# Positions added first on VectorE and gate weights issued later by ScalarE, at the head of a hybrid RG-LRU / GLA / PEER step

## The chip, the cores and the metric

The kernel runs on one core of one Trainium2 chip. The metric is the device time of one execution in microseconds; the time before is the median of three runs, 2560.03 us (2547.81 to 2565.61).

## The reference

One inference step of a two-layer model over 384 tokens of width 1024: 128 prompt tokens and 256 sample tokens. Only the sample tokens get a position table added before the first layer. Layer 0 mixes tokens with a bidirectional RG-LRU, layer 1 with a gated linear attention (GLA), and each layer ends with a PEER mixer that gathers 8 x 16 rows of two tables per token. All of it is float32. What the head of the program computes:

```python
xs = x_sample + grid_pos_embed(rows, D)                 # positions, sample tokens only
mod = silu(cond) @ ada_w[l] + ada_b[l]                  # six vectors of 1024 per layer and kind of token
h = rmsnorm(x, norm1_g) * (1 + scale) + shift           # pre_mod
proj = h @ w_in                                         # RG-LRU: 1024 -> 2048
xr = centred_conv(proj[..., 1024:], conv_w, conv_b)     # four taps
r = sigmoid(block_diag(xr, wa, ba)); i = sigmoid(block_diag(xr, wi, bi))    # gate weights: 16 blocks of 64 x 64
log_a = -8 * r * softplus(-lam)                         # the decay; softplus(-lam) depends on weights alone
a = exp(log_a); b = sqrt(-expm1(2 * log_a)) * (i * xr); h = linear_scan(a, b, h0)
```

## The kernel before, in words

The activations lie feature-major in SBUF: `xT` holds 8 chunks (`C`) of 128 features by 384 tokens. Each engine runs one program written out by hand, in order, and waits on semaphores.

**Weights.** SP streams the large weights as slabs of 1 MB (`stream`, L422): `SEQ` fixes their order (eight `ada` slabs, then `rg_in` 0, four `ada` slabs, `rg_in` 1, and so on) and six slab buffers take turns, so slab k is issued when slab k - 6 has been used. `ada` slabs 0 to 5 go out at once. `ada` 6 and 7 wait for `ada` 0 and 1 to be used.

**TensorE at the head.** `ada_slabs(4)` (L853, four slabs of the modulation product side by side), then `square_sum(0, c)` for the 8 chunks (L878, the norm's sum of squares), then four more `ada` slabs, `ada_columns(0)` (L868, transposes), then `project("rg_in", n)` (L946) for n = 0 to 7 with four `ada` slabs after each second one, then the gate matmuls (L1165), which first wait for all eight loads of gate weights (`bd_in`). A float32 matmul shows as two records in the trace.

**ScalarE at the head.** It issues loads itself: `vec`, `xT`, the position table, `ident`, `iota`, `wz`, and then the gate weights (L539): 8 loads of 128 KB, each in runs of 64 numbers (256 bytes) into the block-diagonal buffer `bd`, behind a wait for that buffer's zeroing. After these come Abs and Exp of lambda (L542, L543), which release VectorE's decay chain; then `squares(0)` (L557) of each chunk of x, the square root (`deviation`, L563), the copy of the first modulation rows (`rows(0)`, L550), `modulate(0)` (L575, writes `hT`) and the copies of the projections out of PSUM into `xpad` (L776, L777).

**VectorE at the head.** First the decay chain (L1227 to L1240): 25 tiny operations on 128 x 16 for softplus(-lam), whose results `dec4` and `ndec8` are first used by ScalarE's Tanh (L796). Then the position adds (L1246, 8 of 128 x 256), each of which releases one of ScalarE's squares; then `norm(0)` (L1274 reciprocal, L1276), `modulation(0)` (L1258, L1268), the zeroing of `xpad` (L1567), and the convolutions (L1571, L1574), one chunk for each copied projection.

**The rest.** Scans, output projection, layer 0's queries, and then, from about 270 us, 768 gathers of 128 rows from each of the two PEER tables, issued by GpSimd and consumed by VectorE (dot products, L1520) and TensorE (weighted sums, L1126), with layer 1's GLA laid in between. A gather waits for indices that VectorE chose.

Of the kernel before, what the change touches and what calls it, by code (L numbers as in the profile page):

```python
# [7 lines left out]
C = D // P  # L8
# [26 lines left out]
for _n in range(TOPK * NT * PH * 2):  # L35
# [3 lines left out]
RG_C = 8.0  # L39
# [6 lines left out]
ALU = mybir.AluOpType  # L46
ACT = mybir.ActivationFunctionType
# [4 lines left out]
V_CW, V_CB, V_BA, V_BI, V_LAM, V_H0, V_BAL, V_GNG, V_FG, V_EPS, V_END = (  # L52
    144, 176, 184, 200, 216, 232, 248, 256, 264, 272, 273)
# [178 lines left out]
def build(nc, x_t, pos_t, vecs, ident_d, mask_d, iota_d, keys_t, ada_w, peer_wq, peer_u, peer_v, rg_w_in,  # L232
          rg_wa, rg_wi, rg_w_out, gla_w_in, gla_w_z, w_alpha, state_gla, gla_w_out, y_t, st_rg, st_gla):
    ctx = ExitStack()
    with ctx:
        def sb(name, shape, dt=F32):
            return ctx.enter_context(nc.sbuf_tensor(name, shape, dt))
# [3 lines left out]
        def sem(name):  # L241
            if name not in sems:
                sems[name] = ctx.enter_context(nc.semaphore(name))
            return sems[name]
# [4 lines left out]
        vec = sb("vec", [P, V_END])  # L249
# [9 lines left out]
        lamv = sb("lamv", [P, 5, 2 * C])  # L259
        dec4 = sb("dec4", [P, 2 * C])  # L260
        ndec8 = sb("ndec8", [P, 2 * C])
# [4 lines left out]
        def part(at, size):  # L266
            return big[:, at:at + size]
# [14 lines left out]
        bd = bd_flat.rearrange("p (k c m) -> p k c m", k=4, c=C)  # L282
# [240 lines left out]
        def _(act):  # L523
            link = Chain(act, sem("act_step"))
# [7 lines left out]
            act.dma_start(ident[:, :], ident_d).then_inc(const_in, 16)  # L532
            act.dma_start(iota16[:, :], iota_d).then_inc(const_in, 16)
            act.dma_start(wz[:, :, :], gla_w_z).then_inc(sem("wz_in"), 16)
            act.wait_ge(sem("bd_zero"), 1)
            for kind, w in enumerate((rg_wa, rg_wi)):
                for d in range(2):
                    for half in range(2):
                        act.dma_start(bd[64 * half:64 * half + 64, 2 * d + kind, :, 64 * half:64 * half + 64],  # L539
                                      w[0, d].rearrange("(c two) i j -> two i c j", two=2)[half]).then_inc(bd_in, 16)  # L540

            link(act.activation(lamv[:, 0, :], vec[:, V_LAM:V_LAM + 2 * C], ACT.Abs))  # L542
            act.activation(lamv[:, 1, :], lamv[:, 0, :], ACT.Exp, scale=-1.0).then_inc(sem("lam_exp"), 1)  # L543

            def rows(group):

                act.wait_ge(sem("ada_used"), 8 * (group + 1))
                if group:
                    act.wait_ge(sem("ada_cols"), group)
                act.activation(ada_rows, bank[5 + group % 3], ACT.Copy).then_inc(sem("ada_rows"), 1)  # L550
# [15 lines left out]
            def modulate(n):  # L566

                k = min(n, 1)
                act.wait_ge(sem("gs_ready"), k + 1)
                for c in range(C):  # L570
                    if c % 2 == 0:
                        act.wait_ge(sem("xn_ready"), 4 * n + c // 2 + 1)
                    for s, (a, b) in enumerate(SEG):
                        if n in (0, 2 - s):
                            act.activation((hP0 if n else hT)[:, c, a:b], xn_p[:, c, :] if n == 2 else xn[:, c, a:b],  # L575
                                           ACT.Identity, scale=gs_of[0][:, k, c, s:s + 1],
                                           bias=mods_of[0][:, 3 * k * C + c, s:s + 1]).then_inc(sem("h_ready"), 1)
# [192 lines left out]
            deviation(0)  # L770
            rows(0)
            modulate(0)
            act.wait_ge(sem("xpad_zero"), 1)
            for n in range(C):
                act.wait_ge(sem("rg_in_mm"), n + 1)
                act.activation(xpad[:, n, PAD_L:PAD_L + TP], bank[n % 4][:, 0:TP], ACT.Copy)  # L776
                act.activation(xpad[:, n, S0 + PAD_L:S0 + PAD_L + TS], bank[n % 4][:, TP:T], ACT.Copy  # L777
                               ).then_inc(sem("rg_in_ev"), 1)
            rows(1)
            for d in range(2):  # L780
                if d == 1:
                    rows(2)
                for kind, dst, col in ((0, g_a[d], V_BA), (1, g_i[d], V_BI)):
                    for c in range(C):
                        n = (2 * d + kind) * C + c
# [436 lines left out]
        def _(dve):  # L1222
            link = Chain(dve, sem("dve_step"))


            dve.wait_ge(sem("lam_exp"), 1)
            e, den, w, w2, s = (lamv[:, i, :] for i in (1, 2, 3, 4, 0))  # L1227
            link(dve.tensor_scalar(den, e, 2.0, None, ALU.add))
            link(dve.reciprocal(den, den))
            link(dve.tensor_tensor(w, e, den, ALU.mult))  # L1230
            link(dve.tensor_tensor(w2, w, w, ALU.mult))
            link(dve.tensor_scalar(s, w2, 1.0 / 17, 1.0 / 15, ALU.mult, ALU.add))
            for k in (13, 11, 9, 7, 5, 3, 1):
                link(dve.tensor_tensor(s, s, w2, ALU.mult))
                link(dve.tensor_scalar(s, s, 1.0 / k, None, ALU.add))
            link(dve.tensor_tensor(s, s, w, ALU.mult))
            link(dve.tensor_scalar(den, vec[:, V_LAM:V_LAM + 2 * C], -1.0, 0.0, ALU.mult, ALU.max))
            link(dve.scalar_tensor_tensor(s, s, 2.0, den, ALU.mult, ALU.add))
            dve.tensor_scalar(ndec8[:, :], s, -RG_C, None, ALU.mult)
            dve.tensor_scalar(dec4[:, :], s, RG_C / 2, None, ALU.mult).then_inc(sem("dec_ready"), 1)  # L1240


            dve.wait_ge(x_in, 16)
            dve.wait_ge(pos_in, 16)
            for c in range(C):
# [3 lines left out]
            def modulation(group):  # L1249

                dve.wait_ge(sem("ada_cols"), group + 1)
                layer = group // 3
                mods = mods_of[layer]
                for i in range(2):
                    m = group % 3 * 2 + i
                    b = vec[:, V_ADAB + layer * 48 + m * C:V_ADAB + layer * 48 + (m + 1) * C]
                    src = bank[4][:, i * SW:(i + 1) * SW].rearrange("p (f s x) -> p s f x", f=2, s=4)[:, :, :, 0:2]
                    ins = dve.tensor_tensor(mods[:, m * C:(m + 1) * C, :].rearrange("p (s f) x -> p s f x", f=2), src,  # L1258
                                            b.rearrange("p (s f) -> p s f", f=2).unsqueeze(3).to_broadcast([P, 4, 2, 2]),
                                            ALU.add)  # L1260
                ins.then_inc(sem("ada_mod"), 1)
                if group % 3 != 1:
                    part = group % 3 // 2
                    dve.wait_ge(sem("ada_mod"), group + 1)
                    col = (V_N1, V_N2)[part]
                    g = vec[:, col + layer * C:col + (layer + 1) * C].unsqueeze(2).to_broadcast([P, C, 2])
                    r = (1 + 3 * part) * C
                    dve.scalar_tensor_tensor(gs_of[layer][:, part, :, :], mods[:, r:r + C, :], 1.0, g, ALU.add,  # L1268
                                             ALU.mult).then_inc(sem("gs_ready"), 1)
# [295 lines left out]
            norm(0)  # L1565
            modulation(0)
            dve.memset(part(6144, C * WPAD), 0.0).then_inc(sem("xpad_zero"), 1)  # L1567
            for c in range(C):
                dve.wait_ge(sem("rg_in_ev"), c + 1)
                cw = [vec[:, V_CW + c * 4 + j:V_CW + c * 4 + j + 1] for j in range(4)]  # L1570
                link(dve.tensor_scalar(xr[:, c, :], xpad[:, c, 0:WX], cw[0], vec[:, V_CB + c:V_CB + c + 1], ALU.mult,  # L1571
                                       ALU.add))
                for j in range(1, 4):
                    ins = dve.scalar_tensor_tensor(xr[:, c, :], xpad[:, c, j:j + WX], cw[j], xr[:, c, :], ALU.mult,  # L1574
                                                   ALU.add)
                    if j < 3:
                        link(ins)
                ins.then_inc(sem("xr_ready"), 1)
# [113 lines left out]
```

## Time and profile before

| | |
|---|---|
| median of three runs | 2560.03 us |
| lowest, highest | 2547.81, 2565.61 us |
| the profiled execution's own time | 2561.2 us |
| its span, first to last instruction | 2558.8 us |
| TensorE busy | 2025.1 us (79%) |
| VectorE busy | 1655.2 us (65%) |
| GpSimd busy | 1625.5 us (64%) |
| ScalarE busy | 525.5 us (21%) |
| mean granted TensorE clock | 0.894 of full speed |

The times below are microseconds from the start of the span. PE is TensorE and PEld its weight loads, DVE is VectorE, ACT ScalarE, POOL GpSimd; a q behind a name (ACTq, SPq) is the issuing of DMAs by that engine, which is not counted as busy. [...] Queue q1 carries what SP issues, q10 what ScalarE issues.

### The profile page before, as it was taken

To read this page: it belongs to the slowest core of one execution; us is meant where nothing else is said; L and a number is where in the kernel's file an instruction comes from. 1 tells how busy PE (TensorE), PEld (TensorE's weight loads), DVE (VectorE), ACT (ScalarE), POOL (GpSimd) and SP (SyncE) were. 2 spreads that over 40 slices of the span, in tenths; PEclk is the share of its full clock that TensorE was granted. 3 is DMA by queue.
4 is the path that set the end of the run, shared out by engine and by line. 5 is a ranking of instruction groups with operands and counts; after the bars stand their busy time and mean duration, and the time that the engine had idled before them with its cause. 6 is when DMAs were issued, how large, how long until landed. Compare 5 with 4: busy or idle time off the path is not lost.

```text
span 2558.8 us, 22158 instructions
## 1 busy us (share of the span) xinstructions
PE 2025.1 (79%) x6920; PEld 1102.8 (43%) x6920; DVE 1655.2 (65%) x4012; ACT 525.5 (21%) x1334; POOL 1625.5 (64%) x1543
## 2 busy tenths in 40 slices
PE   5998897977796767986686887889687776858676
PEld 2557543433342323763464465455333332424233
DVE  2235767787778756578878746576757594665744
ACT  2261211111111112221121221222111111212011
POOL 0000577777777777677776655576777777777773
PEclk8999898988898879897898899999889888988888
DMA  8884799999999999999999989899999999999996
GB/s 293 329 317 183 298 378 407 409 383 409 407 394 406 392 396 362 394 385 335 342 391 347 411 330 397 306 381 351 397 389 410 385 375 398 390 367 386 409 384 253
DMA packets 248098, 938.63 MB, mean 367 GB/s; under 512 B 31344, under 2 KB 35824, under 8 KB 232624
## 3 DMA queue, kind: packets, MB, share of 16 engines
q0 software_dynamic: 221184, 805.40, 81.2%
q1 hardware_dynamic: 19248, 125.32, 12.6%
q10 hardware_dynamic: 7552, 6.51, 0.8%
q8 instruction: 57, 0.93, 0.1%
q14 instruction: 57, 0.47, 0.1%
HBM read 934.49 MB, written 2.63 MB: 366 GB/s over the span
## 4 chain that ended last, share of the span: by engine, by line
PE 31%; POOL 29%; DMA 16%; DVE 11%; issue 11%; ACT 1%; ACTq 1%; SPq 0%; DVEq 0%; POOLq 0%
POOL big L501 22%; PE psum L1126 17%; DMA big<-in_peer_u,idx 14%; POOL big L509 7%; PE psum L946 4%; DVE big L1520 3%; DMA big<-in_peer_v,idx 2%; PE psum L1009 1%; PE psum L968 1%; PE psum L853 1%; PE psum L1049 1%; PE psum L1165 1%; ACTq L539 1%; DVE big L1494 1%; PE psum L894 1%
## 5 line engine op out<-in xcount | busy, mean ns | idle before, releaser
L1126 PE MATMUL psum<-big,diag 128*128 128x512 f32 x2816 | 1317.8, 626 | 387.9 <-ACT diag L764 369.8
L1520 DVE SCALAR_TENSOR_TENSOR big<-big 128x1024 f32<-128x1024 f32 x768 | 932.2, 1225 | 554.3 <-DMA big<-in_peer_u,idx 536.0
L501 POOL DMA_INDIRECT big<-in_peer_u,idx x768 | 823.0, 1072 | 546.0 <-DVE flag L1346 268.2
L1126 PEld LDWEIGHTS psum<-big,diag 128*128 128x128 f32 x2816 | 559.0, 202 | 1095.2 <-issue 1039.6
L509 POOL DMA_INDIRECT big<-in_peer_v,idx x768 | 798.5, 1040 | 357.0 <-issue 191.0
L764 ACT ACTIVATE diag<-ident,wts 128x128 f32<-128x128 f32 x704 | 245.0, 394 | 460.1 <-PE psum L1126 442.5
L754 ACT ACTIVATE tanh<-inner 128x16 f32<-128x16 f32 x48 | 10.4, 216 | 852.4 <-DVE inner L1528 852.4
L968 PE MATMUL psum<-big 128*128 128x128 f32 (+2 forms) x736 | 164.9, 384 | 22.1 <-ACT big L622 13.0
L968 PEld LDWEIGHTS psum<-big 128*128 128x128 f32 x736 | 123.8, 195 | 66.7 <-issue 22.9
L946 PE MATMUL psum<-big 128*128 128x384 f32 (+2 forms) x512 | 133.7, 421 | 9.8 <-DVE big L1607 6.5
L1009 PE MATMUL psum<-big 128*128 128x256 f32 (+1 forms) x768 | 131.5, 332 | 4.0 <-DMA big<-in_gla_w_in 2.3
L1009 PEld LDWEIGHTS psum<-big 128*128 128x128 f32 x768 | 118.6, 194 | 21.3 <-issue 10.7
L946 PEld LDWEIGHTS psum<-big 128*128 128x128 f32 x512 | 89.5, 197 | 51.2 <-issue 14.3
L1494 DVE SCALAR_TENSOR_TENSOR big<-big,wts 128x1024 f32<-128x1024 f32 x63 | 80.9, 1284 | 41.3 <-DMA big<-in_peer_v,idx 37.6
L1520 DVE DVE_READ_ACCUMULATOR big<-big 128x1 f32 x768 | 63.1, 82 | 0.0
L853 PE MATMUL psum<-big,cond 128*2 128x256 f32 x768 | 51.6, 398 | 8.6 <-DMA big<-in_ada_w 8.6
L607 ACT ACTIVATE big<-psum 128x256 f32<-128x256 f32 (+2 forms) x46 | 17.1, 377 | 182.0 <-PE psum L968 182.0
L1049 PE MATMUL psum<-big 128*128 128x256 f32 x192 | 42.4, 379 | 0.0
L1363 DVE SCALAR_TENSOR_TENSOR xT<-psum,mods,xT 128x256 f32<-128x256 f32 (+1 forms) x48 | 17.0, 409 | 36.0 <-PE psum L1019 35.9
L1049 PEld LDWEIGHTS psum<-big 128*128 128x128 f32 x192 | 36.5, 190 | 7.5 <-issue 2.9
L853 PEld LDWEIGHTS psum<-big,cond 128*2 128x2 f32 x768 | 20.6, 87 | 42.2 <-DMA big<-in_ada_w 13.2
L1341 DVE TENSOR_TENSOR onehot<-onehot,i 128x512 f32<-128x512 f32 x48 | 33.3, 693 | 1.6
(192 smaller groups left out, 1308.5 us busy)
## 6 DMA issues: line engine op xcount, KB each, us to landing
big<-in_ada_w SPq DMA_DIRECT2D x48, 1024.0 KB, 8.2
big<-in_peer_wq SPq DMA_DIRECT2D x24, 1024.0 KB, 8.1
big<-in_gla_w_in SPq DMA_DIRECT2D x24, 1024.0 KB, 8.2
big<-in_peer_u,idx POOLq DMA_INDIRECT x768, 6.6
big<-in_peer_v,idx POOLq DMA_INDIRECT x768, 6.8
big<-in_rg_w_in SPq DMA_DIRECT2D x8, 1024.0 KB, 11.1
big<-in_gla_w_out SPq DMA_DIRECT2D x8, 1024.0 KB, 8.5
big<-in_rg_w_out SPq DMA_DIRECT2D x4, 1024.0 KB, 7.1
```

Of the source, the lines that this page charges most:

```text
L501: pool.indirect_dma_start(ubuf[n % US], None, u_rows, bass.IndirectOffsetOnAxis(ap=idx[kept(g)][:, j:j + 1], axis=0)).then_inc(u_in[n % US ...
L509: pool.indirect_dma_start(vbuf[n % VS], None, v_rows, bass.IndirectOffsetOnAxis(ap=idx[kept(g)][:, j:j + 1], axis=0)).then_inc(v_in[n % VS ...
L764: act.activation(diag[k % DS][:, :], ident[:, :], ACT.Copy, scale=wts[g % 3][:, j:j + 1]).then_inc(sem("diag_ready"), 1)
L853: mm = pe.matmul(out[32 * s:32 * s + 2, o:o + SW], cond[:, c, :], slab[SLOT[k]][:, c, :], start=False, stop=(c == C - 1), skip_group_check ...
L946: mm = pe.matmul(out, slab[SLOT[k]][:, c, (n % 2) * P:(n % 2 + 1) * P], rhs[:, c, :], start=(c == 0), stop=(c == C - 1))
L968: mm = pe.matmul(bank[6 + half][:, 0:width], weights[:, c, half * P:(half + 1) * P], rhs[:, c, :], start=(c == 0), stop=(c == C - 1))
L1009: mm = pe.matmul(out[:, j * n:(j + 1) * n], weights[:, c, j % 2 * P:(j % 2 + 1) * P], rhs[:, c, :], start=(c == 0), stop=(c == C - 1), ski ...
L1049: mm = pe.matmul(out[:, t * DV:(t + 1) * DV], s.hT[:, c, t * P:(t + 1) * P], weights[:, c, :], start=(c == 0), stop=(c == C - 1), skip_gro ...
L1126: mm = pe.matmul(acc[t][:, half * 512:(half + 1) * 512], diag[k % DS][:, :], vbuf[n % VS][:, half * 512:(half + 1) * 512], start=False, st ...
L1341: link(dve.tensor_tensor(oh, oh, i12[:, :, :].unsqueeze(2).to_broadcast([P, 2, TOPK, TOPK]), ALU.mult))
L1494: dve.scalar_tensor_tensor(total, vbuf[n % VS], wts[g % 3][:, j:j + 1], total, ALU.mult, ALU.add).then_inc(side_done, 1)
L1520: dve.scalar_tensor_tensor(ubuf[n % US], ubuf[n % US], 0.5, x, ALU.mult, ALU.mult, accum_out=dot[:, j:j + 1]).then_inc(u_free, 1)
```

## The change

On ScalarE, the eight loads of gate weights leave the head. They are issued in pairs behind the copies of projections 0 to 3: `gate_weights(n // 2, n % 2)`. Abs and Exp of lambda move from ahead of the squares to behind `modulate(0)`. On VectorE, the decay chain moves from the start of the program to behind the zeroing of `xpad`, ahead of the first convolution, so the position adds come first.

```diff
@@ ScalarE
-            act.wait_ge(sem("bd_zero"), 1)
-            for kind, w in enumerate((rg_wa, rg_wi)):
-                for d in range(2):
-                    for half in range(2):
-                        act.dma_start(bd[64 * half:64 * half + 64, 2 * d + kind, :, 64 * half:64 * half + 64],
-                                      w[0, d].rearrange("(c two) i j -> two i c j", two=2)[half]).then_inc(bd_in, 16)
-
-            link(act.activation(lamv[:, 0, :], vec[:, V_LAM:V_LAM + 2 * C], ACT.Abs))
-            act.activation(lamv[:, 1, :], lamv[:, 0, :], ACT.Exp, scale=-1.0).then_inc(sem("lam_exp"), 1)
+
+            def gate_weights(kind, d):
+
+                w = (rg_wa, rg_wi)[kind]
+                if (kind, d) == (0, 0):
+                    act.wait_ge(sem("bd_zero"), 1)
+                for half in range(2):
+                    act.dma_start(bd[64 * half:64 * half + 64, 2 * d + kind, :, 64 * half:64 * half + 64],
+                                  w[0, d].rearrange("(c two) i j -> two i c j", two=2)[half]).then_inc(bd_in, 16)
...
             modulate(0)
+            link(act.activation(lamv[:, 0, :], vec[:, V_LAM:V_LAM + 2 * C], ACT.Abs))
+            act.activation(lamv[:, 1, :], lamv[:, 0, :], ACT.Exp, scale=-1.0).then_inc(sem("lam_exp"), 1)
             act.wait_ge(sem("xpad_zero"), 1)
             for n in range(C):
                 act.wait_ge(sem("rg_in_mm"), n + 1)
...
                                ).then_inc(sem("rg_in_ev"), 1)
+                if n < 4:
+                    gate_weights(n // 2, n % 2)
             rows(1)
@@ VectorE
             link = Chain(dve, sem("dve_step"))
-
-
-            dve.wait_ge(sem("lam_exp"), 1)
-            e, den, w, w2, s = (lamv[:, i, :] for i in (1, 2, 3, 4, 0))
...
-            dve.tensor_scalar(ndec8[:, :], s, -RG_C, None, ALU.mult)
-            dve.tensor_scalar(dec4[:, :], s, RG_C / 2, None, ALU.mult).then_inc(sem("dec_ready"), 1)
...
             dve.memset(part(6144, C * WPAD), 0.0).then_inc(sem("xpad_zero"), 1)
+            dve.wait_ge(sem("lam_exp"), 1)
+            e, den, w, w2, s = (lamv[:, i, :] for i in (1, 2, 3, 4, 0))
...
+            dve.tensor_scalar(ndec8[:, :], s, -RG_C, None, ALU.mult)
+            dve.tensor_scalar(dec4[:, :], s, RG_C / 2, None, ALU.mult).then_inc(sem("dec_ready"), 1)
             for c in range(C):
                 dve.wait_ge(sem("rg_in_ev"), c + 1)
```

The order on ScalarE from its last small load to the square root, before: gate weights (`in_rg_wa`, `in_rg_wi`) and lambda (`lamv`) stand ahead of the squares (L557).

```order
L534 DMA wz<-in_gla_w_z 128x256
L539 DMA big<-in_rg_wa 64x8x64 x4
L539 DMA big<-in_rg_wi 64x8x64 x4
L542 ACTIVATE lamv<-vec 128x16
L543 ACT_TABLE_LOAD
L543 ACTIVATE lamv<-lamv 128x16
L557 ACTIVATE big<-xT 128x384 x8
L563 ACT_TABLE_LOAD
```

The same stretch of ScalarE in the changed kernel:

```order
L533 DMA iota<-in_iota 128x16
L534 DMA wz<-in_gla_w_z 128x256
L557 ACTIVATE big<-xT 128x384 x8
L563 ACT_TABLE_LOAD
L563 ACTIVATE sd<-psum,vec 128x384
```

The squares follow the last small load directly.

ScalarE in the changed kernel from the end of `modulate(0)` (last row of L575) to the fourth projection's copies (L778 and L779, which are L776 and L777 before):

```order
L575 ACTIVATE big<-big,mods,gs 128x256
L773 ACTIVATE lamv<-vec 128x16
L774 ACT_TABLE_LOAD
L774 ACTIVATE lamv<-lamv 128x16
L778 ACTIVATE big<-psum 128x128
L779 ACTIVATE big<-psum 128x256
L542 DMA big<-in_rg_wa 64x8x64 x2
L778 ACTIVATE big<-psum 128x128
L779 ACTIVATE big<-psum 128x256
L542 DMA big<-in_rg_wa 64x8x64 x2
L778 ACTIVATE big<-psum 128x128
L779 ACTIVATE big<-psum 128x256
```

Lambda with its table load now stands between the modulation and the first copy, and two loads stand behind each of the first copies (two more pairs, of `in_rg_wi`, follow).

VectorE's first rows before, from the decay chain's last operations (`ndec`, `dec`) to the zeroing of `xpad` (L1567) and the first convolution:

```order
L1239 TENSOR_SCALAR ndec<-lamv 128x16
L1240 TENSOR_SCALAR dec<-lamv 128x16
L1246 TENSOR_TENSOR xT<-xT,big 128x256 x8
L1274 RECIPROCAL rstd<-sd 128x384
L1276 TENSOR_TENSOR big<-xT,rstd 128x768 x4
L1258 TENSOR_TENSOR mods<-psum,vec 128x16 x2
L1268 SCALAR_TENSOR_TENSOR gs<-mods,vec 128x16
L1567 MEMSET big 128x3120
L1571 TENSOR_SCALAR big<-big,vec 128x387
```

VectorE's first rows in the changed kernel, as far as the decay chain's first operations:

```order
L1233 TENSOR_TENSOR xT<-xT,big 128x256 x8
L1261 RECIPROCAL rstd<-sd 128x384
L1263 TENSOR_TENSOR big<-xT,rstd 128x768 x4
L1245 TENSOR_TENSOR mods<-psum,vec 128x16 x2
L1255 SCALAR_TENSOR_TENSOR gs<-mods,vec 128x16
L1554 MEMSET big 128x3120
L1557 TENSOR_SCALAR lamv<-lamv 128x16
L1558 RECIPROCAL lamv<-lamv 128x16
```

The adds are VectorE's first work, and the whole chain stands between the zeroing and the first convolution. TensorE's and SP's own orders are the same in both kernels.

## Rows read from the trace of the kernel before

**Rows 1.** The page: chain that ended last, share of the span by engine

```profile
PE 31%; POOL 29%; DMA 16%; DVE 11%; issue 11%; ACT 1%; ACTq 1%; SPq 0%; DVEq 0%; POOLq 0%
```

**Rows 2.** Chain of waits, 0 to 130 us: start, length, what

```profile
10.11 12.83 ACTq L539
```

**Rows 3.** Waits, 0 to 60 us: us in total, times, longest

```profile
DVE lamv L1228 <- ACT lamv L543: 29.8, 1, 29.8
```

**Rows 4.** Timeline, 0 to 100 us: start, length, engine, line, count [idle before]

```profile
1.68 0.45 ACTq L527 DMA_DIRECT2D big<-in_pos_t  x1
...
7.97 14.97 ACTq L539 DMA_DIRECT2D big<-in_rg_wa  x4
...
20.31 6.49 PE L853 MATMUL psum<-big,cond 128*2 128x256 f32 x58 [1.70 <-DMA big<-in_ada_w]
...
28.06 0.22 ACT L542 ACTIVATE lamv<-vec 128x16 f32<-128x16 f32 x1 [21.23 <-issue]
...
34.67 2.77 DVE L1246 TENSOR_TENSOR xT<-xT,big 128x256 f32<-128x256 f32 x8
35.12 3.41 ACT L557 ACTIVATE big<-xT 128x384 f32<-128x384 f32 x8 [5.32 <-DVE xT L1246]
...
35.70 7.45 PE L878 MATMUL psum<-big,ones 128*128 128x384 f32 x16 [8.90 <-ACT big L557]
...
43.08 3.64 PE L853 MATMUL psum<-big,cond 128*2 128x256 f32 x64
...
47.51 0.65 PE L868 MATMUL psum<-ident,small 128*128 128x128 f32 x4 [0.80 <-ACT small L550]
...
49.87 0.24 DVE L1258 TENSOR_TENSOR mods<-psum,vec 128x16 f32<-128x16 f32 x2
...
51.49 13.23 PE L946 MATMUL psum<-big 128*128 128x384 f32 x32 [3.32 <-ACT big L575]
...
59.65 0.28 ACT L776 ACTIVATE big<-psum 128x128 f32<-128x128 f32 x1 [2.17 <-PE psum L946]
...
69.26 10.59 PE L946 MATMUL psum<-big 128*128 128x384 f32 x32
```

**Rows 5.** DMA issues, 0 to 120 us: KB, median us to landing

```profile
xT<-in_x_t ACTq DMA_DIRECT2D x1, 1536.0 KB, 11.6
big<-in_pos_t ACTq DMA_DIRECT2D x1, 1024.0 KB, 16.1
```

**Rows 6.** Windows: length, busy of PE, PEld, DVE, ACT, POOL, granted clock, DMA share, GB/s

```profile
26.80:29.70 2.90, 0.00 (x1) 0.00 (x0) 0.00 (x0) 1.61 (x3) 0.00 (x0) 0.98 1.24 225
...
35.70:39.90 4.20, 4.20 (x7) 2.38 (x8) 1.74 (x6) 4.12 (x8) 0.00 (x0) 0.51 1.04 395
...
64.70:114.00 49.30, 49.22 (x357) 25.64 (x356) 16.45 (x28) 5.64 (x16) 0.00 (x0) 1.00 0.89 337
```

**Rows 7.** Line 853, 20.3 to 26.8 us: ns min/median/max, first and last start

```profile
L853 PE MATMUL psum<-big,cond x58: 379/631/631, 20.3 to 26.4; 128*2 128x256 f32 x58
```

**Rows 8.** Line 422, issued 26.0 to 27.2 us: two slabs, landing min/median/max

```profile
L422 SPq DMA_DIRECT2D big<-in_ada_w x2: 327/467/607, 26.4 to 26.8; - x2
...
DMA to landing us min/median/max: 6.7/7.9/9.0
```

**Rows 9.** Line 422, issued 66 to 71 us: three slabs, landing

```profile
L422 SPq DMA_DIRECT2D big<-in_ada_w x3: 328/431/1104, 69.3 to 70.9; - x3
...
DMA to landing us min/median/max: 5.0/8.2/9.5
```

**Rows 10.** DMA queue, 24 to 28 us: packets, MB, share of 16 engines

```profile
q10 hardware_dynamic: 2607, 0.68, 105.4%
```

**Rows 11.** DMA queues, 32 to 36 us

```profile
q1 hardware_dynamic: 207, 1.50, 94.9%
q10 hardware_dynamic: 207, 0.05, 6.7%
```

**Rows 12.** Timeline, 100 to 400 us: the first gate matmuls

```profile
114.18 8.73 PE L1165 MATMUL psum<-big 128*128 128x387 f32 x26
```

More of the change, by code:

```diff
@@ L1223, in _ @@
             link = Chain(dve, sem("dve_step"))
-            dve.wait_ge(sem("lam_exp"), 1)
-            e, den, w, w2, s = (lamv[:, i, :] for i in (1, 2, 3, 4, 0))
[L1228 to L1238, printed above, removed]
-            dve.tensor_scalar(ndec8[:, :], s, -RG_C, None, ALU.mult)
-            dve.tensor_scalar(dec4[:, :], s, RG_C / 2, None, ALU.mult).then_inc(sem("dec_ready"), 1)
             dve.wait_ge(x_in, 16)
@@ L1567, in _ @@
             dve.memset(part(6144, C * WPAD), 0.0).then_inc(sem("xpad_zero"), 1)
+            dve.wait_ge(sem("lam_exp"), 1)
+            e, den, w, w2, s = (lamv[:, i, :] for i in (1, 2, 3, 4, 0))
+            link(dve.tensor_scalar(den, e, 2.0, None, ALU.add))
+            link(dve.reciprocal(den, den))
+            link(dve.tensor_tensor(w, e, den, ALU.mult))
+            link(dve.tensor_tensor(w2, w, w, ALU.mult))
+            link(dve.tensor_scalar(s, w2, 1.0 / 17, 1.0 / 15, ALU.mult, ALU.add))
+            for k in (13, 11, 9, 7, 5, 3, 1):
+                link(dve.tensor_tensor(s, s, w2, ALU.mult))
+                link(dve.tensor_scalar(s, s, 1.0 / k, None, ALU.add))
+            link(dve.tensor_tensor(s, s, w, ALU.mult))
+            link(dve.tensor_scalar(den, vec[:, V_LAM:V_LAM + 2 * C], -1.0, 0.0, ALU.mult, ALU.max))
+            link(dve.scalar_tensor_tensor(s, s, 2.0, den, ALU.mult, ALU.add))
+            dve.tensor_scalar(ndec8[:, :], s, -RG_C, None, ALU.mult)
+            dve.tensor_scalar(dec4[:, :], s, RG_C / 2, None, ALU.mult).then_inc(sem("dec_ready"), 1)
             for c in range(C):
```

## The prediction

> **What bounds the kernel now.** I read the page first. Its chain of the work that ended last is spread over PE 31%, POOL 29% and DMA 16%, with ScalarE's issuing at 1% [rows 1]: nearly all of the time lies in the gathers of the body, which the change does not touch. What it touches is the first 115 us, so I read the chain of waits, the waits and the timeline there. The reader is to see one queue. ScalarE issues the gate weights from 7.97 on, and one of these issues alone is held for 12.83 us [rows 2, 4]. Lambda starts behind them at 28.06, after 21.2 us in which ScalarE computes nothing [rows 4]; VectorE's decay chain waits 29.8 us for it [rows 3]; and TensorE, done with its first four slabs at 20.31 + 6.49 = 26.80, waits 8.9 us for the first square, until 35.70 [rows 4]. Behind the head, from 64.7 to 114, TensorE is busy 49.22 of 49.30 us [rows 6]. What it gains earlier is therefore carried into that stretch whole, unless slabs come late in it.
>
> **The squares come earlier.** In the changed kernel VectorE's adds wait for x and the positions alone. The positions land 16.1 us after their issue at 1.68, at 17.8; x, issued ahead of them, needs 11.6 [rows 4, 5]. Adds take 2.77 us, and squares run from 0.45 us behind the first add for 3.41 us [rows 4]: 18.25 to about 21.7, when ScalarE has long been free (7.97, where the gate weights stood). So VectorE is 17 us earlier, but TensorE gets only 8.9 of them: until 26.80 it is at its slabs. Gain in the start of the sums of squares: 35.70 - 26.80 = 8.9 us.
>
> [...] Which level holds at 26.80? The slab matmuls ahead of it had a median of 631 ns, but the shortest, at the phase's end, took 379 ns [rows 7], and the granted clock stayed at 0.98 until 29.7 with TensorE idle [rows 6]. I take the upper level: 26.8 to 32.1. Bounds: 34.3 (as before) and 36.4 (all slow).
>
> [...]
>
> **The second four slabs** are the next late thing. Two of them are issued only when the first two are used, at 26.4 and 26.8, and landed 6.7 and 9.0 us later [rows 8], at 33.1 and 35.8, while gate packets took 105.4% of the DMA engines' time from 24 to 28 [rows 10]. Without those I go by three slabs elsewhere: the first 5.0 us after 69.3, the last 9.5 us after 70.9 [rows 9], that is 74.3 and 80.4, 3.05 us apart each. So 26.4 + 5.0 = 31.4 and 34.4; late bound 35.8. The phase needs all four from its first chunk, so it runs 34.4 + 3.64 = 38.0. From its end before, 43.08 + 3.64 = 46.72, to the transposes' end at 47.51 + 0.65 = 48.16 were 1.44 us [rows 4]: the modulation could start at 39.5.
>
> VectorE's own path to it, from the sums' end (35.70 + 7.45 = 43.15) to 49.87, took 6.7 us [rows 4] through the square root, the reciprocal and the norm: 32.1 + 6.7 = 38.8. The slabs end last, 39.5. Gain: 49.87 - 39.5 = 10.4 us. Bounds: slabs at 35.8 give 40.9, a gain of 9.0; slow sums give 36.4 + 6.7 = 43.1, a gain of 6.8.
>
> **The first projections** took 13.23 us where later pairs took 10.59 [rows 4], after 3.32 us in which TensorE had nothing to do, of which some 2 us remain (transposes to 39.4, first matmul 1.6 us behind the modulation). I keep 13.23. If the clock does not drop this time, the pair is still paced by the modulation on ScalarE; at most 13.23 - 10.59 = 2.6 us more could be gained. I count 0.
>
> **Lambda on ScalarE** (two activations and a table load, from 28.06 to the end of VectorE's wait at 29.8, so 1.8 us [rows 3, 4]) falls into ScalarE's 2.17 us of idle ahead of the first copy [rows 4]: 0. Uncovered it would delay a copy, for which TensorE has four banks. **The decay chain** on VectorE, from 29.8 to the first add at 34.67, so 4.9 us [rows 3, 4], now delays the first convolution by about 4 us. VectorE is busy 16.45 of 49.30 us there [rows 6], and the gate matmuls ask for the result at 114.18 [rows 12]: 0. Without that cover it would cost 4.9.
>
> **The gate loads** cost twice. Issuing: 2 per copy, 8 in all, on an engine busy 5.64 of 49.30 us [rows 6]; even a hold of 12.83 us [rows 2] behind the fourth copy would only make the fifth copy some 4 us late, long before 114. Cost 0. Queued behind them are the next copies, for which VectorE waits. Moving: 2607 packets took 4 us when they had the engines [rows 10], so 8 loads of 512 packets take 6.3 us. The first pair falls into an idle stretch, the other three among slabs that TensorE takes as they land. Beside slabs, each queue got 207 packets in 4 us, and the small ones took 6.7% of the time [rows 11]: over the 11 us or so of one slab round, 0.7 us. Bounds: nothing, and three quarters of 6.3 = 4.7 us. I take 0.5, nearest to the row of two queues side by side.
>
> **Sum.** 10.4 - 0.5 = 9.9 us, so the profiled execution's 2561.2 becomes 2551.3. The median of the runs shown is 1.2 lower, 2560.03; from it I forecast 2550.1. All later work hangs on this chain (the first gather waits for indices), so I let the body move as a block.
>
> **Rivals.**
>
> [...]
>
> [...]
>
> [...]
>
> *The body gives the gain back.* Gathers and clock in the body vary by themselves (three equal runs lie 17.8 us apart), and the end could sit where it was: 2560. For it: POOL and DMA hold 45% of the chain [rows 1]. Against it: the first gather cannot start before the indices, which move with the head.
>
> *The change doesn't do what it says.* If x or the positions landed later than now, the adds would wait. It takes 9 us of delay to matter at all; I give it nothing of its own.
>
> **How the numbers follow.** Forecast 0.72, less gain 0.13, gain given back 0.10, late gate weights 0.05. Its own range, from the bounds, is a gain of 6 to 13, so 2547 to 2554; three equal runs lie within about 9 us of their middle, and that is wider than the bounds. I take 2538 to 2563. About 1%, 25 us, is what a measurement of this kernel can tell from no change. No case reaches 25 us on either side; what I leave there is for scatter and for what I overlooked. So faster 0.03, within 0.95, slower 0.02.
>
> **What would show it.** Right: the squares on ScalarE start near 18, the sums of squares near 26.8 and last 5 to 6 us; the modulation starts near 39.5 and the first gate matmul at about 104; TensorE has no wait ahead of it. Wrong: sums of 7 us or more (clock), a wait of the second slab phase beyond 35, waits of over 1 us for `ada` slabs between 55 and 104, or a wait for gate weights ahead of L1165's successor; or a first gather some 10 us earlier with the same end.

## The result, and the profile after

The changed kernel took 2536.70 us (median of 12 runs, 2526.50 to 2552.13) where the kernel before, timed beside it, took 2554.39 (12 runs, 2540.42 to 2565.61). The ratio, which is worked out from all runs of both and is not the quotient of the two medians (0.9931), is 0.9943, 95% interval [0.9918, 0.9968]: 14.6 us less, between 8 and 21. Timed again on another occasion it was 0.9933 [0.9907, 0.9960], 17 us less, between 10 and 24. The forecast was 2550.1 from a median of 2560.03, that is 0.9961 of it. The bare 2536.70 lies 1.3 us below the stated range; on the 2560.03 from which that range was made, 0.9943 gives 2545.4, inside it. By the bound of 1% this is the "within" case.

The timeline of the changed kernel's head, which answers to [rows 4] (start, length, engine, line; L882 is L878 of before, L857 is L853, L950 is L946, L1169 is L1165):

```profile
18.11 2.77 DVE L1233 TENSOR_TENSOR xT<-xT,big 128x256 f32<-128x256 f32 x8 [18.11 <-DMA big<-in_pos_t]
18.57 3.41 ACT L557 ACTIVATE big<-xT 128x384 f32<-128x384 f32 x8 [11.45 <-DVE xT L1233]
20.59 6.01 PE L857 MATMUL psum<-big,cond 128*2 128x256 f32 x58 [1.71 <-DMA big<-in_ada_w]
...
26.54 5.43 PE L882 MATMUL psum<-big,ones 128*128 128x384 f32 x16
...
33.50 3.62 PE L857 MATMUL psum<-big,cond 128*2 128x256 f32 x58 [1.00 <-DMA big<-in_ada_w]
...
38.68 0.25 DVE L1245 TENSOR_TENSOR mods<-psum,vec 128x16 f32<-128x16 f32 x2
...
40.31 12.12 PE L950 MATMUL psum<-big 128*128 128x384 f32 x32 [1.85 <-ACT big L575]
...
52.36 1.12 PE L849 MATMUL psum<-zrow 1*128 1x512 f32 x2
...
68.76 3.62 PE L857 MATMUL psum<-big,cond 128*2 128x256 f32 x58 [0.66 <-DMA big<-in_ada_w]
...
86.22 5.30 PE L857 MATMUL psum<-big,cond 128*2 128x256 f32 x58 [1.73 <-DMA big<-in_ada_w]
...
105.57 8.73 PE L1169 MATMUL psum<-big 128*128 128x387 f32 x26
```

The reader is to see two halves. Up to 52 us TensorE gains. The sums of squares start at 26.54 behind the slabs, without a wait, where before TensorE waited until 35.70. The modulation comes at 38.68 instead of 49.87 (11.2 us earlier), and the first pair of projections ends at 40.31 + 12.12 = 52.4 instead of 51.49 + 13.23 = 64.7 (12.3 earlier). From there it loses: the first gate matmul comes at 105.57 instead of 114.18, only 8.6 earlier. Between these stand two waits for `ada` slabs, 0.66 and 1.73 us, and a slab phase of 5.30 us where 3.62 is usual. A second profile of the changed kernel repeats this (waits of 0.81 and 1.97 us, the phase behind the second 4.98 us, the first gate matmul at 106.17), and three more profiles of the kernel before have their first gate matmul at 113.24, 112.92 and 111.99. So the gain at that point is 5.8 to 8.6 us, by the pair of profiles that is taken, and the pair shown here gives the most.

The granted clock at the first projections, in before and then in the changed kernel, and around the second of these waits, from the windows view (columns as in [rows 6]):

```profile
51.40:55.50 4.10, 4.01 (x7) 2.21 (x8) 2.18 (x1) 4.10 (x10) 0.00 (x0) 0.50 1.00 424
```

```profile
39.20:45.00 5.80, 4.69 (x11) 1.79 (x12) 2.66 (x1) 5.80 (x14) 0.00 (x0) 1.00 1.01 414
...
85.00:90.00 5.00, 3.78 (x44) 1.58 (x48) 0.94 (x2) 0.00 (x0) 0.00 (x0) 0.69 0.66 274
...
88.00:89.00 1.00, 1.00 (x16) 0.39 (x12) 0.00 (x0) 0.00 (x0) 0.00 (x0) 0.50 0.24 98
```

At the projections the clock stayed at 1.00, where before it had fallen to 0.50. Just after the wait that ended at 86.2 it fell too (0.50 from 87 to 90), and that is why the slab phase there took 5.30 us: from 87 to 90 a slab matmul took 634 ns (median), and 379 in the phase at 68.76. So the clock fell behind a wait, and it was back at 1.00 by 91.4 under the slab matmuls. How much of a wait it takes the rows don't show: TensorE waited 1.73 us ahead of 86 and the clock fell, and 1.85 us ahead of 40 and it stayed.

The first gather of the body, in before's timeline and then in the changed kernel's:

```profile
272.73 1.08 POOL L501 DMA_INDIRECT big<-in_peer_u,idx  x1 [268.19 <-DVE flag L1346]
```

```profile
263.63 1.08 POOL L501 DMA_INDIRECT big<-in_peer_u,idx  x1 [259.09 <-DVE flag L1333]
```

The head is 9.1 us shorter in this pair of profiles. The profiled spans differ by 34.7 (2558.8 and 2524.1), so the bodies by 25.6; the experiments show how much of that is scatter.

### The profile page after: what moved, and what is told of

Read it like the earlier page. It is cut to its first block, busy times and chain, and to the rows that moved or that the text cites. A ratio compares the mean times of both kernels' runs of the same rounds, so it can differ in the third digit from the quotient of the medians.

```text
span 2524.1 us, 22158 instructions
## 1 busy us (share of the span) xinstructions
PE 2018.8 (80%) x6920; PEld 1098.8 (44%) x6920; DVE 1655.6 (66%) x4012; ACT 525.2 (21%) x1334; POOL 1608.7 (64%) x1543
## 4 chain that ended last, share of the span: by engine, by line
PE 32%; POOL 28%; DMA 17%; issue 11%; DVE 11%; ACT 1%; SPq 0%; DVEq 0%; ACTq 0%; POOLq 0%
POOL big L501 22%; PE psum L1130 19%; DMA big<-in_peer_u,idx 14%; POOL big L509 6%; PE psum L950 4%; DVE big L1507 3%; PE psum L972 2%; DMA big<-in_ada_w 2%; PE psum L857 2%; PE psum L1013 1%; PE psum L1053 1%; DMA big<-in_peer_v,idx 1%; PE psum L1169 1%; ACT diag L764 1%; PE psum L898 1%
## 5 line engine op out<-in xcount | busy, mean ns | idle before, releaser
L501 POOL DMA_INDIRECT big<-in_peer_u,idx x768 | 811.3, 1056 | 533.5 <-DVE flag L1333 259.1
L950 PE MATMUL psum<-big 128*128 128x384 f32 (+2 forms) x512 | 131.8, 415 | 9.0 <-DVE big L1609 7.1
L950 PEld LDWEIGHTS psum<-big 128*128 128x128 f32 x512 | 87.2, 193 | 50.8 <-issue 11.3
L857 PE MATMUL psum<-big,cond 128*2 128x256 f32 x768 | 53.0, 406 | 11.7 <-DMA big<-in_ada_w 11.7
L857 PEld LDWEIGHTS psum<-big,cond 128*2 128x2 f32 x768 | 20.8, 89 | 46.4 <-DMA big<-in_ada_w 16.4
## 6 DMA issues: line engine op xcount, KB each, us to landing
big<-in_rg_w_in SPq DMA_DIRECT2D x8, 1024.0 KB, 11.2
```

The lines of the kernel that those rows point to most:

```text
L501: pool.indirect_dma_start(ubuf[n % US], None, u_rows, bass.IndirectOffsetOnAxis(ap=idx[kept(g)][:, j:j + 1], axis=0)).then_inc(u_in[n % US ...
L857: mm = pe.matmul(out[32 * s:32 * s + 2, o:o + SW], cond[:, c, :], slab[SLOT[k]][:, c, :], start=False, stop=(c == C - 1), skip_group_check ...
L950: mm = pe.matmul(out, slab[SLOT[k]][:, c, (n % 2) * P:(n % 2 + 1) * P], rhs[:, c, :], start=(c == 0), stop=(c == C - 1))
```

## The experiments

Two questions are open. Which of the two moves, ScalarE's or VectorE's, made the gain? And what took back 3.7 us between 52 and 106: the gate packets among the slabs, or a TensorE that now outruns its slab stream? A third came up on the way: what holds ScalarE's issues. The edits are shown shortened, with words in parentheses in place of code. Each profile is of one execution; where a timeline ends at 112 us, the length of its last row is cut there.

**VectorE's order alone.** ScalarE as before.

```diff
 (ScalarE)  gate weights, Abs and Exp of lambda, then squares(0), as before
-(VectorE)  dve.wait_ge(sem("lam_exp"), 1); decay chain; position adds; ...; memset(xpad)
+(VectorE)  position adds; ...; memset(xpad); dve.wait_ge(sem("lam_exp"), 1); decay chain
```

> Only VectorE's order is changed; ScalarE issues gate weights and lambda ahead of the squares as before. Theory (ScalarE's issue queue is what held the head): the adds run near 18, but the squares cannot start before ScalarE is through with lambda at 29.8; sums of squares from about 30.4 at the lower clock, 7.4 us, modulation near 44.5 (5.3 us earlier than before's 49.9), first gate matmul near 109, total ratio to before about 0.998. Rival (VectorE's chain ahead of the adds was the cause): squares near 18, modulation near 39, first gate matmul near 105, as in the changed kernel.

Ratio 0.9991 [0.9964, 1.0018]. The chain of waits to 50 us, and then the timeline of this kernel:

```profile
22.86 2.90 ACTq L539
...
27.16 8.79 ACTq L539
```

```profile
17.73 2.77 DVE L1231 TENSOR_TENSOR xT<-xT,big 128x256 f32<-128x256 f32 x8 [17.73 <-DMA big<-in_pos_t]
22.86 13.09 ACTq L539 DMA_DIRECT2D big<-in_rg_wi  x4
24.83 0.81 SPq L422 DMA_DIRECT2D big<-in_ada_w  x2
...
37.65 3.39 ACT L557 ACTIVATE big<-xT 128x384 f32<-128x384 f32 x8
```

The rival falls: the adds ran at 17.73, but the squares stayed behind ScalarE's issues, and nothing was gained. In this profile the head even got longer (first gather at 278.20, 272.73 before). The theory's numbers fall too: squares were due at 29.8 and came at 37.65, because the last gate load's issue was held for 8.79 us (0.66 in the profile of before). Slabs 6 and 7 were issued from 24.83 on, 2.3 us ahead of it; in before it was 0.9 us ahead (from 26.4 [rows 8], with the last gate load at 27.36 in the chain of waits). The timed ratio may mix executions with this hold and without it, so it says little about the order by itself.

**ScalarE's order alone.** Gate weights as in the changed kernel, lambda ahead of the squares, VectorE as before.

```diff
+            link(act.activation(lamv[:, 0, :], vec[:, V_LAM:V_LAM + 2 * C], ACT.Abs))
+            act.activation(lamv[:, 1, :], lamv[:, 0, :], ACT.Exp, scale=-1.0).then_inc(sem("lam_exp"), 1)
             squares(0)
 (VectorE)  decay chain first, then the position adds, as before
```

> Gate weights late as in the changed kernel, lambda on ScalarE ahead of the squares (about 8 to 10 us), VectorE's order as before. Theory: lambda and the decay chain then lie under the wait for the positions, so squares start near 18.5, modulation near 38.7 and the first gate matmul within 1 us of the changed kernel's 105.6; total ratio to before 0.993 to 0.997. Rival (VectorE's order matters): first gate matmul later than 108.

Its timeline:

```profile
38.40 0.25 DVE L1260 TENSOR_TENSOR mods<-psum,vec 128x16 f32<-128x16 f32 x2
...
105.80 6.46 PE L1169 MATMUL psum<-big 128*128 128x387 f32 x19
```

The head is the changed kernel's within 0.3 us, first gather at 263.41: in these profiles ScalarE's move is the whole gain of the head, and VectorE's order is not needed once lambda is early, since chain and lambda then lie under the wait for the positions. The ratio was 0.9978 [0.9949, 1.0007], 0.0008 above the band that was expected, with an interval that holds both the band and no change.

**All gate loads behind the squares**, ahead of the square root.

```diff
             squares(0)
+            for n in range(4):
+                gate_weights(n // 2, n % 2)
+            (Abs and Exp of lambda)
             deviation(0)
```

> VectorE as changed; the eight gate loads and lambda stand on ScalarE right behind the squares, ahead of the square root. Theory (gate packets among the slabs cost the 3.7 us that the changed kernel lost between 52 and 106): the packets now pass from 22 to 29, slabs 6 and 7 land at 33 to 36, modulation at 39.5 to 41, but no wait over 0.7 us for ada slabs between 55 and 104, first gate matmul at 103 to 105. Rival (TensorE, now earlier, outruns the slab stream by itself): the waits stay and the first gate matmul is at 106 or later.

The chain of waits to 50 us, and the timeline:

```profile
27.25 8.64 ACTq L542
```

```profile
45.67 0.25 DVE L1245 TENSOR_TENSOR mods<-psum,vec 128x16 f32<-128x16 f32 x2
...
74.71 3.63 PE L857 MATMUL psum<-big,cond 128*2 128x256 f32 x64
...
108.26 4.17 PE L1169 MATMUL psum<-big 128*128 128x387 f32 x12
```

Two things came together. The last issue was held again, 8.64 us, and with it the square root, so the modulation came at 45.67 and not at 40. But the slab waits are gone: only one of 0.18 us is left between 55 and 108. From the modulation to the first gate matmul were 108.26 - 45.67 = 62.6 us, as against 105.57 - 38.68 = 66.9 in the changed kernel: 4.3 us less, as the theory has it. The first gate matmul itself missed its 103 to 105 because of the hold. And because the hold made TensorE late here, which gave the slab stream time, this run alone does not exclude the rival. Ratio 0.9969 [0.9945, 0.9993].

**Four gate loads behind each of copies 0 and 1.**

```diff
-                if n < 4:
-                    gate_weights(n // 2, n % 2)
+                if n < 2:
+                    gate_weights(n, 0)
+                    gate_weights(n, 1)
```

> As the changed kernel, but four gate loads behind copy 0 and four behind copy 1. Theory (gate packets among slabs): most packets pass between 48 and 57 where the DMA engines had room, the waits for ada slabs at 68 and 86 shrink to under 0.7 us, first gate matmul at 102 to 104, 2 to 3.5 us ahead of the changed kernel; in the total (0.1%) not to be told from it. Rival (the slab stream by itself): first gate matmul at 105 to 106 again.

> Four gate loads behind each of copies 0 and 1, timed beside the changed kernel on the same chip. Theory: the head is 4 us shorter than the changed kernel's, so 0.9985 of its time, inside the intervals; the profile shows the first gate matmul near 101.5 again, as against 105.6. Rival (its 101.5 was a chance of timing): 104 or more.

The timeline of the first of these runs, its DMA queue from 55 to 60 us, and the first gate matmul of the second:

```profile
68.19 3.62 PE L858 MATMUL psum<-big,cond 128*2 128x256 f32 x58 [1.05 <-DMA big<-in_ada_w]
...
83.31 3.63 PE L858 MATMUL psum<-big,cond 128*2 128x256 f32 x64
...
101.55 8.74 PE L1170 MATMUL psum<-big 128*128 128x387 f32 x26
```

```profile
q10 hardware_dynamic: 2112, 0.52, 59.2%
```

```profile
102.89 8.73 PE L1170 MATMUL psum<-big 128*128 128x387 f32 x26
```

2112 packets of ScalarE's queue, half of the gate loads, pass between 55 and 60, and the other half before 55. The wait at 68 is not smaller than in the changed kernel (1.05 and 0.66), but the wait at 86 with its fall of the clock is gone, and the first gate matmul comes 2.7 to 4.0 us earlier than the changed kernel's 105.57. Part of that is an earlier start: the first slab phase happened to end sooner, and the modulation came at 37.42 and 37.92 where it was 38.68. Counted from the modulation, 64.1 and 65.0 us passed as against 66.9, so the move of the loads itself is worth 1.9 to 2.8 us. In the second run a wait of 1.40 us stood at 99 instead, with no fall of the clock. "Under 0.7 us" is missed, "102 to 104" is met or bettered, "near 101.5 again" is missed by 1.4 us, and both rivals fall. The total does not show it. Ratios to before were 0.9966 [0.9940, 0.9993] and 0.9958 [0.9932, 0.9985]; the changed kernel, timed on the same occasion as the second, was at 0.9933 [0.9907, 0.9960].

**No gate loads at all.**

```diff
-                if n < 4:
-                    gate_weights(n // 2, n % 2)
 (TensorE)
-            pe.wait_ge(bd_in, 16 * 8)
+            pe.wait_ge(sem("bd_zero"), 1)
```

> The eight gate loads are left out, so the gate matmuls work on zeros (the gates' results are not the reference's); only the head up to the first gate matmul is read. Theory (gate packets among slabs): no wait over 0.7 us for ada slabs between 55 and 104 and no fall of the granted clock there, first gate matmul at 102 to 102.5. Rival (the slab stream by itself): waits near 68 and 86 as in the changed kernel, first gate matmul near 105.6.

The timeline:

```profile
97.91 3.62 PE L855 MATMUL psum<-big,cond 128*2 128x256 f32 x58 [0.24 <-DMA big<-in_ada_w]
101.45 8.74 PE L1167 MATMUL psum<-big 128*128 128x387 f32 x26
```

No wait over 0.24 us is left in the stretch, and the first gate matmul is at 101.45. The modulation came at 38.77, as in the changed kernel, so this comparison has no earlier start in it. That settles the second question: the gate loads cost the changed kernel's head 105.57 - 101.45 = 4.1 us. Counted from the modulation it is 4.2, and 5.2 against the changed kernel's second profile. The rival, a TensorE that outruns its slabs by itself, falls.

**The hold.** Is the kernel before, in other executions, held like the first and third experiments? It was profiled three times more.

> The kernel before, unchanged, profiled once more. The run with VectorE's order alone (and the one with gates behind the squares) held the last gate load's issue for about 8.7 us, where before's profile shows 0.66. Theory: the hold comes by chance of timing, when the first four slabs are done early and slabs 6 and 7 are issued before ScalarE's last gate load; so before has it in some executions. Each profile then shows one of two: first slab phase ends after 26.5 and the last gate issue takes 0.7 (first square near 35), or it ends before 26 and the issue is held 8 to 9 us (first square 42 to 44). Rival: the adds at 18 cause the hold; before's profile is like the first one, whenever its slab phase ends.

> As b1: one of the two pictures, by the end of the first slab phase (theory), or always the short issue (rival).

> As b1: one of the two pictures, by the end of the first slab phase (theory), or always the short issue (rival).

| | first slab phase ends | slabs 6, 7 issued from | last gate issue, at and length | squares start | first gather | span | span less first gather |
|---|---|---|---|---|---|---|---|
| before | 26.80 | 26.42 | 27.36, 0.66 | 35.12 | 272.73 | 2558.8 | 2286.1 |
| first | 26.73 | 26.35 | 27.13, 0.66 | 34.90 | 271.68 | 2544.7 | 2273.0 |
| second | 26.29 | 25.90 | 27.21, 0.94 | 35.25 | 271.86 | 2541.0 | 2269.1 |
| third | 26.15 | 25.77 | 27.06, 0.85 | 35.03 | 270.77 | 2543.8 | 2273.0 |

None ended its slab phase before 26, so these three cannot tell the theories apart; the two with the slabs 1.3 us ahead of the last gate load show a little of a hold (0.94 and 0.85), while 2.1 to 2.3 us ahead made 8.64 and 8.79. The count of slabs goes along with the lead: two or three had been issued ahead of that load in these four, and four in the two held profiles, so the lead and the count can't be told apart. The profiles show something else: heads within 2 us of each other, and bodies (last column) that differ by 17.

Next the slabs were taken out of the way: VectorE's order alone, as in the first experiment, with one wait in SP.

```diff
 (SP, stream)
+                    if k == SLABS + 2:
+                        sp.wait_ge(sem("lam_exp"), 1)
                     if BEFORE[k] is not None:
                         wait_used(BEFORE[k])
```

> VectorE's order alone, as in the first experiment, and SP issues slab 6 only when ScalarE is through with lambda. Theory (slabs issued first hold the last gate load): the last gate issue takes under 1 us, lambda near 28 to 30, squares start at 30 instead of 37.6, sums near 30.5; the second slab phase waits for slabs 6 and 7, which land 5 to 9 us behind 30. Rival (the adds cause the hold): the hold of 8 to 9 us stays.

The chain of waits to 60 us, and the timeline:

```profile
27.12 0.66 ACTq L541
```

```profile
20.28 5.23 PE L855 MATMUL psum<-big,cond 128*2 128x256 f32 x58 [1.68 <-DMA big<-in_ada_w]
...
29.48 3.40 ACT L559 ACTIVATE big<-xT 128x384 f32<-128x384 f32 x8
29.59 0.80 SPq L424 DMA_DIRECT2D big<-in_ada_w  x2
30.03 0.30 PEld L880 LDWEIGHTS psum<-big,ones 128*128 128x128 f32 x2 [5.03 <-ACT big L559]
```

The slab phase ended early here (25.5), the adds ran early, and the last issue took 0.66 all the same. With the slabs issued behind it, at 29.59, it was not held: by this profile it is the slabs ahead of it, and not the early adds, that hold it. The squares came at 29.48, as the first theory had wanted, and the first gather at 264.81. What holds the fourth gate load is another matter: its issue took 12.74 to 12.83 us in every profile in which the gate loads stood at the head, this one included, and 0.66 us where they were issued behind the squares, from 20.7 on. Which of the loads ahead of it held it is not shown.

At last the same wait in the kernel before, timed, since it would gain if before were often held.

```diff
 (SP, stream, everything else as before)
+                    if k == SLABS + 2:
+                        sp.wait_ge(sem("lam_exp"), 1)
```

> The kernel before, with SP issuing slab 6 only when ScalarE is through with lambda, so that the last gate load cannot be held behind slabs 6 and 7. Without a hold these slabs still land near 35 and 38, ahead of the second slab phase at 43, so the head is that of before's profiles (first gather at 271 to 273). Theory (before is held in most of its timed executions, though in none of four profiles, which would make the changed kernel's gain 15 us where the profiles' heads show 8 to 9): ratio to before 0.996 to 0.998. Rival (before is seldom held; the rest of the gain is scatter of the body): 0.999 to 1.001.

Its timeline:

```profile
20.35 4.93 PE L855 MATMUL psum<-big,cond 128*2 128x256 f32 x58 [1.70 <-DMA big<-in_ada_w]
...
29.70 0.81 SPq L424 DMA_DIRECT2D big<-in_ada_w  x2
```

Ratio 0.9992 [0.9972, 1.0012], inside the rival's band, though the interval reaches into the theory's. First gather at 271.54, as in before's profiles. But the first slab phase, up to whose end this kernel does what before does, ended at 25.28, as early as in the two held profiles. Without the added wait slabs 6 and 7 would have gone out some 2.3 us ahead of the last gate load (an estimate: in the first experiment slab 6 went out 0.38 us before the phase's end, and the last gate load is at 27.23 here). So executions of before that meet the condition of the hold do occur. How many is not shown: a hold costs some 8 us (an estimate from its length), and the ratio allows a gain of 2 us, at most 7. That leaves anything from no held execution to most of them, and how much of the timed gain beyond the head is hold stays open too.

**The changed kernel again.**

> The changed kernel, unchanged, timed beside the kernel before and beside the variant with four gate loads behind each of two copies. Theory (the head is what moves, and before's head comes in two forms, about 9 and about 17 us later than this one's): ratio 0.994 to 0.9965. Rival (body scatter alone made the first ratio 0.9943): 0.9965 or above.

Ratio 0.9933 [0.9907, 0.9960], slightly below the theory's band, with the first gather at 263.75 and a span of 2541.1, so a body of 2277.4 us (2260.5 in the first profile). Five profiles of before's head (with the last experiment's) have bodies of 2261 to 2286, two of the changed kernel 2261 and 2277. The profiles show no difference of the bodies, only their scatter of some 25 us. Their heads (first gather 270.77 to 272.73 before, 263.63 and 263.75 after) differ by 7.0 to 9.1 us. Yet both timings gave more (14.6 and 17 us) than that, and the second interval, 10 to 24 us, does not reach down to it. The kernel with ScalarE's move alone, whose head is the same, gave 0.9978, which is 5.6 us. The intervals overlap. Where the further 5 to 10 us come from (held executions of before, the body, or chance) stays open.

## Why the prediction was right, and where it was not

*The sums of squares come earlier by 8.9 us.* Right: 26.54 without a wait, predicted 26.8. The adds waited for the positions until 18.11 (17.8), and TensorE's first four slabs set the start. The first two experiments show that ScalarE's queue, and not VectorE's order, was what held them.

*The sums at the upper level, 5.3 us.* Right: 5.43, with a granted clock of 1.00 from 26.5 to 32, so the clock was up behind the slab matmuls, as the 379 ns of [rows 7] said. The 5.3 is 16 records of 10.59 / 32 = 0.33 us [rows 4]. The late bound, 36.4, is 26.8 + 16 x 0.60, from seven records in 4.20 us at 0.51 [rows 6]; no run shows all sixteen at that level, and the longest sums took 8.05 us (VectorE's order alone, from 38.21). The other sign, the granted 0.98 of [rows 6], was weaker than it looked: the same column reads 1.00 from 20.3 to 26.8, where most records still took 631 ns.

*The second four slabs end last, modulation at 39.5.* Right in kind, 0.8 us too late. The landing of the two slabs in the changed kernel, which answers to [rows 8]:

```profile
L422 SPq DMA_DIRECT2D big<-in_ada_w x2: 328/380/431, 26.2 to 26.6; - x2
...
DMA to landing us min/median/max: 4.8/5.8/6.9
```

They landed at 31.0 and 33.5, where 31.4 and 34.4 were taken. TensorE waited 1.00 us for the later one, as the forecast's order of events has it. But VectorE's path, with its norm until 38.7, came to the modulation last: the two ends were 0.7 us apart in the forecast, and their order turned.

*The first projections, counted at 0.* Too careful: they took 12.12, not 13.23, with the clock at 1.00 where it had been 0.50. That is 1.1 us, inside the 2.6 stated as the bound. The idle ahead of them was shorter (1.85 us, 3.32 before), but whether that kept the clock up is not shown: with four gate loads behind each of two copies the idle was 1.75 us, and the clock fell all the same, in the first of its two profiles:

```profile
40.00:42.00 2.00, 2.00 (x4) 0.91 (x5) 1.14 (x1) 2.00 (x6) 0.00 (x0) 0.57 1.05 442
```

*The gate loads, 0.5 us.* This step failed in size. They cost 4.1 us by the experiment without them (up to 5.2 against the second profile of the changed kernel); the stated bound was 4.7. The step took "nearest to the row of two queues side by side", [rows 11], in which slab packets stood against few small ones. The changed kernel's queues from 70 to 75 us:

```profile
q1 hardware_dynamic: 157, 1.13, 71.2%
q10 hardware_dynamic: 1413, 0.35, 40.8%
```

The small packets took 40.8% of the time, not 6.7%. And they did so while TensorE's next slabs were on their way: the slab that ended the wait at 86 took 13.3 us in the chain of waits. The rows that fitted better were those of 24 to 28 us [rows 10], where the gate packets had the engines nearly to themselves and the next slabs had only just been issued. The wait then cost twice, because the clock fell behind it: 5.30 instead of 3.62 us. A wait was priced as a wait; its second price, the clock, was left out of the sum.

*TensorE busy 49.22 of 49.30 us behind the head.* The reading was that TensorE does not wait there, but the share hides waits that the weight loads show. The slab phase at 79.78 of before took 4.26 us and not 3.63, and so did the one at 95.54:

```profile
80.43 3.11 PEld L853 LDWEIGHTS psum<-big,cond 128*2 128x2 f32 x58 [0.55 <-DMA big<-in_ada_w]
```

So slabs came 0.55 us late twice in that profile already, and the slab stream had nothing in hand for the gate packets.

*The sum.* 12.3 gained and 3.7 lost make 8.6 at the first gate matmul and 9.1 at the first gather, where 9.9 was forecast: two errors, 1.9 us more at the start and 3.2 us more lost, which partly cancelled. That the head came out near 9.9 is in part luck; over all profiles it is 7.0 to 9.1. Whether the body moved as a block, the profiles with their scatter of 25 us can't show, and the timed gain of 14.6 and 17 us is larger than anything in this sum.

*The rivals.* Gate weights that land late (0.05) did not come about: in the changed kernel they were issued from 47.4 to 68.2 and landed 3.4 to 11.7 us after their issue, and the first gate matmul followed its slab phase directly. Less gain (0.13) by a lower clock at the sums did not come about either (5.43 us at 1.00), though a fall of the clock did cost 1.7 us later, at 86. Lambda and the decay chain cost nothing, as said: the first convolution started at 52.81 behind the chain, and the second followed it at once.

## What to carry to other kernels

Small loads that an engine issues ahead of its own arithmetic hold that arithmetic for as long as the issue is held, and this can be more than ten times what one issue takes (12.8 and 8.6 us, as against 0.66); put them behind the first work that others wait for. When they are moved, ask what they meet in the new place: the best place found by the first gate matmul, though the total did not show it, was one where half of the gate loads were issued (46.5 to 49.2) before the next slabs (from 51.5), and the price of meeting a stream that is taken as it lands is the wait (1.73 us at 86) and, where it falls, the clock behind it (5.30 us for a slab phase of 3.62). Where a change moves 9 us of 2550 and the body scatters by 25, read the gain from the stage's own landmarks, here the first gate matmul and the first gather.

## What the runs showed of the hardware that was not expected

The issue of the eighth gate load, 512 runs of 256 bytes, took 0.66 to 0.94 us when another engine's slabs of 1 MB were issued behind it or the first of them up to 1.3 us ahead of it (two or three slabs), and 8.6 to 8.8 us when the first went out 2.1 to 2.3 us ahead (four slabs). So about 1 us in the end of the first slab phase (25.2 and 25.6 in the two held profiles, 26.2 to 26.8 in those of before) goes with the difference. The first slab phase itself ended anywhere between 25.2 and 26.8 us in kernels that were the same up to there, with its matmuls changing from 631 to 379 ns at a point that varies from execution to execution (the median of its 58 records is 631 ns in before, where it ended at 26.80, and 380 in the first experiment, where it ended at 25.2). The granted clock does not show that change: it reads 1.00 from 20.3 to 26.8 in before. What sets the point is not shown.
